# Output projection and first MLP unit of the second layer by token tile, and a later last query unit

## The reference

```python
# layer i = 1 of second_block
q, k, v = split_cols(h @ w, (ATT_QW, ATT_KVW, ATT_KVW))          # 16 query heads, 4 key heads, 64 wide
q = axial_rope(split_heads(q, ATT_Q_HEADS), row, col)            # a rotation by position
...
y = merge_heads(window_attention(q, k, v, k_c, v_c, od_sink[j])) @ od_w_out[j]   # 1024 x 1024
x = layer_norm(DEEPNORM_ALPHA * x + g1 * y, ln_g[i, 0], ln_b[i, 0])
m = jnp.square(jax.nn.relu((x * (1.0 + sc2) + sh2) @ mlp_w1[i])) @ mlp_w2[i]     # 1024 -> 4096 -> 1024
x = layer_norm(DEEPNORM_ALPHA * x + g2 * m, ln_g[i, 1], ln_b[i, 1])
```

## Time and profile before

| | |
|---|---|
| median of 3 runs | 1339.11 us |
| lowest and highest | 1335.56 and 1345.13 us |
| the profiled execution, its device time | 1340.16 us |
| its span in the trace | 1338.4 us |
| mean granted clock of TensorE | 0.991 |
| busy: PE, PEld, DVE, ACT, POOL | 97%, 90%, 66%, 43%, 8% |
| instructions | 24359 |

### The profile page before, as it was taken

How to read it: one execution, slowest core, us unless ns; L and a number is a source line. 1 busy time by engine, 2 the same in 40 slices (tenths; PEclk the granted TensorE clock), 3 DMA queues, 4 the chain that set the end, 5 groups by cost and what they waited for, 6 DMA issues and landing times.

```text
span 1338.4 us, 24359 instructions
## 1 busy us (share of the span) xinstructions
PE 1292.9 (97%) x10441; PEld 1205.1 (90%) x10441; DVE 883.2 (66%) x1357; ACT 579.2 (43%) x892; POOL 102.9 (8%) x153
## 2 busy tenths in 40 slices
PE   5899999999999999999999999999999899899997
PEld 4799998899988788899998898998999899899997
DVE  3567755557544466467677687676778886767566
ACT  4434445543665544526422313213155664445431
POOL 0111100000001111000000011111100120000000
PEclk9899999999989999999999999999999999999999
DMA  9897886445244544032444356575434202555550
GB/s 349 307 332 233 264 241 181 142 146 161 93 128 161 187 153 163 33 121 101 148 150 158 115 173 202 172 236 190 127 127 158 64 1 64 170 191 191 183 180 33
DMA packets 163881, 218.40 MB, mean 163 GB/s; under 512 B 6030, under 2 KB 141589, under 8 KB 163638
## 3 DMA queue, kind: packets, MB, share of 16 engines
q1 hardware_dynamic: 140196, 148.11, 33.7%
q0 software_dynamic: 22880, 67.42, 16.0%
q10 hardware_dynamic: 698, 1.32, 0.3%
HBM read 215.70 MB, written 1.12 MB: 162 GB/s over the span
## 4 chain that ended last, share of the span: by engine, by line
PE 84%; DVE 7%; DMA 4%; ACT 3%; issue 2%; POOL 0%; SPq 0%; DVEq 0%; ACTq 0%
PE bank L1322 30%; PE bank L694 11%; PE bank L713 10%; PE bank L746 7%; PE bank L729 4%; DMA strip_b<-distance_parts 2%; PE bank L1399 2%; PE bank L1226 2%; PE bank L887 2%; PE bank L805 2%; PE bank L1414 1%; PE bank L1300 1%; DVE wlo L2079 1%; DMA graw_b<-in_w_mod 1%; PE bank L998 1%
## 5 line engine op out<-in xcount | busy, mean ns | idle before, releaser
L2079 DVE TENSOR_TENSOR wlo<-raw,whi 128x2048 fp32r<-128x2048 f32 x131 | 297.4, 2275 | 93.5 <-ACT whi L1493 93.2
L1493 ACT ACTIVATE whi<-raw 128x2048 fp32r<-128x2048 f32 x131 | 247.9, 1898 | 194.7 <-PE bank L1322 130.9
L1322 PE MATMUL bank<-whi,m_hi 128*128 128x256 f32 x576 | 160.4, 278 | 1.2 <-DVE m_lo L2677 0.8
L1322 PE MATMUL bank<-whi,m_lo 128*128 128x256 f32 x576 | 159.7, 277 | 0.0
L1322 PE MATMUL bank<-wlo,m_hi 128*128 128x256 f32 x576 | 159.7, 277 | 0.0
L1322 PE MATMUL bank<-a_hi,whi 128*128 128x256 f32 (+1 forms) x448 | 148.5, 332 | 0.0
L1322 PE MATMUL bank<-a_lo,whi 128*128 128x256 f32 (+1 forms) x448 | 148.1, 331 | 0.0
L1322 PE MATMUL bank<-a_hi,wlo 128*128 128x256 f32 (+1 forms) x448 | 148.0, 330 | 0.0
L1322 PEld LDWEIGHTS bank<-whi,m_hi 128*128 128x128 f32 x576 | 108.5, 188 | 1.9 <-DVE m_lo L2677 1.2
L1322 PEld LDWEIGHTS bank<-whi,m_lo 128*128 128x128 f32 x576 | 108.3, 188 | 0.0
L1322 PEld LDWEIGHTS bank<-wlo,m_hi 128*128 128x128 f32 x576 | 108.1, 188 | 0.1
(11 more groups left out here) (439 smaller groups left out, 3335.3 us busy)
## 6 DMA issues: line engine op xcount, KB each, us to landing
raw<-in_mlp_w SPq DMA_DIRECT2D x64, 1024.0 KB, 5.2
raw<-in_w_in SPq DMA_DIRECT2D x32, 1024.0 KB, 7.2
graw_b<-in_w_mod POOLq DMA_DIRECT2D x64, 512.0 KB, 4.9
raw<-in_ev_w_in SPq DMA_DIRECT2D x12, 1024.0 KB, 5.1
pre<-in_w_ada SPq DMA_DIRECT2D x16, 512.0 KB, 9.8
graw_a<-in_w_mod POOLq DMA_DIRECT2D x16, 512.0 KB, 7.1
Y<-in_w_mod POOLq DMA_DIRECT2D x16, 512.0 KB, 4.2
raw<-in_od_w_qkv SPq DMA_DIRECT2D x6, 1024.0 KB, 4.8
```

The source lines that it names most:

```text
L1322: mm = nc.tensor.matmul(o, x, y, start=(k == 0 and i == 0), stop=(k == KT - 1 and i == 2))
L1493: nc.scalar.activation(split_pair(u, kt * cols)[0], landing(u, kt * cols), ACT.Copy).then_inc(hi_done, 1)
L2079: nc.vector.tensor_tensor(split_pair(u, n)[1], landing(u, n), bf(whi[u % HI], n), ALU.subtract).then_inc(lo_done, 1)
```

## The change

In the attention loop the last query unit moves. DVE rotates its two tiles in steps 4 and 5 (before: 1 and 3), PE transposes it in step 7 (before: 4), ACT and DVE round it in step 7 (before: 4). Its transpositions go to bank 0 instead of bank 1, so they wait for the first `window_out`, and the product with the values waits at `n` = 2 and `n` = 4 for what it did not wait for before.

After the attention, work goes by token tile. The projection is done as eight results of 24 matmuls, one for each unit and tile (`od_tile`); tile 0 of all four units comes first. Tile 0 is normalised while PE multiplies tile 1, its eight transpositions (`turn_tile(0)`) stand between the second and third result of tile 1, and the first MLP unit is multiplied for tile 0 (`first_hidden(0)`) before tile 1 is transposed, then for tile 1. That unit is therefore 96 matmuls of 128 columns instead of 48 of 256. `Y` rows 1 and 3 take the two normalised tiles, and `n_hi`, `n_lo` (in the place of `a_lo`) take what `a_hi`, `a_lo` took. ACT and DVE do their passes for each tile (`affine_tile`, `low_tile`: 128 x 128 instead of 128 x 256, twice as many), and the statistics for each tile and unit (`od_stats`). The splits of the weights change places too: `U_M1` and `U_M1 + 1` come between the tiles (the latter on DVE in four quarters, `quarter_lo`), and `U_M1 + 2` on ACT comes after tile 1's passes. The projection's weight buffers are all in use until tile 1 is multiplied, so `freed` for `U_OD` is four results later.

```diff
         for c0 in range(0, D, UC):
-            add(a["od_w_out_2"][0], c0, UC, 1)
+            add(a["od_w_out_2"][0], c0, UC, 2)
...
+        in_halves(U_OD, 4)
...
-        PAIRS, L_BANK, TQ_BANK = QH // 2 * NT, ((4, 5), (2, 3)), (6, 7, 0, 1)
+        PAIRS, L_BANK, TQ_BANK = QH // 2 * NT, ((4, 5), (2, 3)), (6, 7, 0, 0)
...
# PE, in transpose_q and window_values
+                if j == 3:
+                    pe.wait_ge(wa_o, 1)
...
-                if n < 4:
-                    pe.wait_ge(kq_ev, KVH + 3 + g)
+                if n in (0, 4):
+                    pe.wait_ge(kq_ev, KVH + 3 + g // 2)
+                elif n == 2:
+                    taken(pe, before[U_QKV + 5])
                 elif n % 2 == 0:
                     pe.wait_ge(wa_o, g - 1)
...
# PE, the attention loop
-                if n in (2, 4):
-                    transpose_q(1 + n // 2)
+                if n in (2, 7):
+                    transpose_q(2 if n == 2 else 3)
...
# PE, projection to MLP: all of it new
+            def first_hidden(m):
...
+                for n in range(2):
+                    for k in range(KT):
+                        if n == 0:
+                            pe.wait_ge(tr_lo, LN_T0[4] + KT * m + k + 1)
+                        for i, (w, x) in enumerate(((wh, n_hi), (wl, n_hi), (wh, n_lo))):
+                            mm = nc.tensor.matmul(bank[bk(b)][:, n * S + m * P:n * S + (m + 1) * P], w[:, k, n * P:(n + 1) * P],
+                                                  x[:, k, ms], start=(m + n + k + i == 0), stop=(k == KT - 1 and i == 2),
+                                                  skip_group_check=True)
...
+            for j in range(4):
+                od_tile(j, 0)
+            od_tile(0, 1)
+            od_tile(1, 1)
+            turn_tile(0)
+            od_tile(2, 1)
+            od_tile(3, 1)
+            first_hidden(0)
+            turn_tile(1)
+            first_hidden(1)
...
# ACT
-                if n in (3, 4):
-                    take_transposed(3 + n)
+                if n in (3, 7):
+                    take_transposed(6 if n == 3 else 7)
...
-            for u in range(U_OD, U_M1):
-                split_hi(u + LEAD)
-            tile_roots(4)
-            affine_half(4, 0)
+            split_hi(U_OD + LEAD)
+            tile_root(4, 0)
+            split_hi(U_M1)
+            act.wait_ge(aff_done, 3 + LN_CALL.index(4))
+            affine_tile(0)
+            split_hi(U_M1 + 1)
+            tile_root(4, 1)
+            affine_tile(1)
+            split_hi(U_M1 + 2)
...
# DVE
-                if n == 1:
-                    query_rows(3, (0,))
...
-                if n in (3, 4):
-                    low_transposed(3 + n)
-                if n == 3:
-                    query_rows(3, (1,))
+                if n in (3, 7):
+                    low_transposed(6 if n == 3 else 7)
+                if n in (4, 5):
+                    query_rows(3, (n - 4,))
...
+            split_lo(U_OD + LEAD)
+            for j in range(4):
+                od_stats(j, 0)
+            tile_norm(0)
+            od_stats(0, 1)
+            split_lo(U_M1)
+            od_stats(1, 1)
+            for k in range(KT):
+                low_tile(0, k)
+            od_stats(2, 1)
+            od_stats(3, 1)
+            tile_norm(1)
+            for k in range(KT):
+                low_tile(1, k)
+                if k % 2:
+                    quarter_lo(U_M1 + 1, k // 2)
+            split_lo(U_M1 + 2)
             residual(2, 0)
             residual(2, 1)
```

More of the change, by code:

```diff
@@ L273, in build @@
             o_hi, o_lo = [flat(a_hi)[:, i * 2048:(i + 1) * 2048].rearrange("p (k n) -> p k n", k=KT) for i in range(2)]
+            n_hi, n_lo = [flat(a_lo)[:, i * 2048:(i + 1) * 2048].rearrange("p (k n) -> p k n", k=KT) for i in range(2)]
             sink, nsink = stat[:, 44:60], stat[:, 24:40]
@@ L1456, in _ @@
             pe.wait_ge(wa_o, PAIRS // 2)
[L1457 to L1464, removed]
-                for k in range(KT):
[L1466 to L1469, removed]
@@ L1470, in _, with od_tile @@
-            for m in range(NT):
+            def od_tile(j, m):
+                u, b = U_OD + j, place[U_OD + j, m]
+                wh, wl = [w.rearrange("p (k n) -> p k n", k=KT) for w in split_pair(u)]
+                pe.wait_ge(lo_done, u + 1)
+                pe.wait_ge(free[bk(b)], nth(b))
+                for k in range(KT):
+                    for i, (w, x) in enumerate(((wh, o_hi), (wh, o_lo), (wl, o_hi))):
+                        mm = nc.tensor.matmul(bank[bk(b)][:, 0:UC], x[:, k, m * P:(m + 1) * P], w[:, k, :],
+                                              start=(k == 0 and i == 0), stop=(k == KT - 1 and i == 2))
+                mm.then_inc(tile_done, 1)
@@ L1477, in _ @@
-            col_half(U_M1, 0, a_hi, a_lo, before[U_M1], t0=LN_T0[4])
-            M1_ARGS = (U_M1, a_hi, a_lo, S, *half_m, 32, False)
+                    nc.tensor.transpose(bank[4 + k // 2][:, (k % 2) * S + m * P:(k % 2) * S + (m + 1) * P],
+                                        Y[:, 2 * m + 1, k * P:(k + 1) * P], ident).then_inc(tr_full, 1)
+            def first_hidden(m):
+                u, b = U_M1, before[U_M1]
+                wh, wl = [w.rearrange("p (k n) -> p k n", k=KT) for w in split_pair(u)]
+                pe.wait_ge(lo_done, u + 1)
+                if m == 0:
+                    pe.wait_ge(free[bk(b)], nth(b))
+                ms = slice(m * P, (m + 1) * P)
+                for n in range(2):
[6 more added lines that the diff above has]
+                                                  skip_group_check=True)
+                if m:
+                    mm.then_inc(tile_done, 1)
@@ L2059, in _ @@
             mlp(U_M1, S, half_m[0], 32, 3, lead=8 - LEAD)
-            tile_roots(6)
+            for m in range(NT):
+                tile_root(6, m)
         @block_.vector
@@ L2856, in _, with od_stats @@
             affine(4, 2, M1 + 24, M1 + 32).then_inc(aff_done, 1)
-            for u in range(U_OD, U_M1 - 1):
-                split_lo(u + LEAD)
-                gated_stats(before[u], grow[5][:, 0], xres, u - U_OD, 0, ALPHA)
-            for m in range(NT):
-                if m == 0:
-                    dve.wait_ge(od_half, 1)
-                b = before[U_M1 - 1]
-                tile_stats((take(b) if m else bank[7])[:, 0:UC], grow[5][:, 0], m, ALPHA, b if m else None)
-            for m, finished in enumerate((ln_even, ln_odd)):
+            def od_stats(j, m):
+                b = place[U_OD + j, m]
+                tile_stats(take(b)[:, 0:UC], grow[5][:, 0], m, ALPHA, b, j)
```

61 lines of the change are left out of this document (43 added, 18 removed).

## The result

The changed kernel takes 1342.22 us (median of 20 runs, 1338.74 to 1345.12) against 1339.25 us for the kernel before (20 runs, 1335.56 to 1345.13). The ratio is 1.002, 95% interval 1.0011 to 1.0029: 2.7 us slower, 1.5 to 3.9. By the measure of 1% that is no change. The profiled execution has 1342.75 us, its span 1340.9 us.

The account below looks back on a forecast made before the run. PE has 84% of the chain, but ACT and DVE hold up the start of the MLP. 1340.16 - 1.1 (attention) + 2.8 (projection to MLP) = 1341.9 us profiled, 1340.8 us median; range 1335.5 to 1345.0.

Parts of the forecast that it names:

- (a): Projection to MLP: PE fills its wait and becomes the bound, faster; -3.9 with the attention, 1335.2 us; chance 0.1.
- The attention: Attention loop: PE no longer waits for the second rotation, gains 1.9 us, gives part back; -1.1 us, between 0 and -1.9.
- The prices: Projection to MLP: 0.111 us per 128-column matmul, 0.59 per ACT `k` of 128 columns, 1.4 per tile and unit of statistics.
- rival (b): `affine_tile(1)`: tile 1's passes cost ACT what 256 columns cost; +1.4 us on the forecast, 1342.2; chance 0.12.
- rival (e): Second transpositions: the norm of tile 1 is what is late, 128-column matmuls being cheap; 1339.4 us; chance 0.08.
- The first square: Start of the MLP: first square 42.4 us after the projection's start instead of 39.64, +2.8 us.
- the term: Projection to MLP: +2.8 us; ends +1.3 (norm of tile 1 late) and +4.2 (ACT's passes at the 256-column price).
- Those 2.7 us are PE's slack.: MLP unit 4: PE ready near 58.0 us after projection start, fourth hidden unit at 60.7, so PE does not delay it.
- rival (c): `first_hidden(1)`: TensorE at its lower clock, 1.2 GHz, slower; 60 such matmuls give +3.3 us on the forecast, 1344.1; chance 0.06.
- Behind 1178.47 the change moves nothing: From the second part of MLP unit 4 on, where the chain returns to PE for good: no change in time.
- (d): Attention: DVE is late in every step and all the gain is given back; +1.1 us on the forecast, 1341.9; chance 0.14.

Follow-up runs that it names:

- wide_narrow: Changed kernel with the first MLP unit multiplied over all 256 columns ahead of tile 1's turn, then over tile 1's 128 behind it; ratio 1.0015.
- narrow_wide: Changed kernel with the first MLP unit multiplied over tile 0's 128 columns (thrown away), then over all 256 behind tile 1's turn; ratio 1.0001.
- att_only: Kernel before with the attention part of the change alone (last query unit rotated and transposed later); 1336.27 us, ratio 0.9986.
- reorder: Changed kernel, 96 narrow matmuls kept, with the rounding of `U_M1 + 2` and the two residual calls moved into idle ACT and DVE time; ratio 1.0023.
- wide_twice: Changed kernel with its 96 matmuls in the same places but each over 256 columns, the first 48 thrown away; ratio 1.0012.

## Why the prediction was right, and where it was wrong

The predicted time, 1340.8 us, lies 1.4 us under the median, within the range, and the class (no change by 1%) is the measured one. The forecast difference was +1.7 us, the measured one is +2.7. That the number came so near is partly luck: by the dates of the first profile of either kernel the change costs 4.5 us from the first logits on, mostly because one step failed. And the range was set by the scatter of three executions; every rival but (a) lay inside it too, so it could not have told them apart.

**The attention: right.** Predicted -1.1 us, measured -0.91 against the first profile. Counted from the first logits, the product with the values of pair 0 starts 1.76 us earlier than before (1.9 predicted), that of pair 2 1.60 us, and that of pair 3, which stands behind the transpositions of step 7, 1.22 us: the gain and most of what is given back are where the prediction had them. Not foreseen was that the removed wait is also one behind which the clock can fall (-2.5 then).

**The prices: right.** The 128-column matmul was put at 0.111 us and took 5.31 / 48 = 0.111. By the 81 ns of the Trainium skill, "TensorE: Matmul & The Clock Gate", section "Back-to-back issue gap", a tile would take an estimated 3.9 us; the measured 5.31 us decides against it for these matmuls. ACT's `k` over 128 columns was put at 0.59 us and took 0.54 (1148.23 to 1148.77), so rival (b) was wrong. The norm of tile 1 was put at S + 26.9 and was ready at 1144.29, S + 26.8; PE came at S + 28.4 (predicted 28.2), so rival (e) did not happen. The first square was put at S + 42.4 and came at 42.0. One end of the term was added up wrongly: with the norm late at S + 26.9 instead of 28.2 it would be +1.5, not +1.3. Nothing else rests on it.

**The step that failed: "Those 2.7 us are PE's slack."** It held PE at 2.4 GHz. PE should have ended `first_hidden(1)` at S + 37.3 and ended at S + 40.3; the three hidden units took 18.43 us where 144 x 0.115 = 16.6 were counted. Together 4.8 us, 2.7 of them slack, so 2.1 on the path: the second part of unit 4 starts at 62.8 instead of 60.7. That is rival (c), which had a chance of 0.06. Its mechanism was described rightly, and its arithmetic (slack first, then the path) too; it was judged unlikely by the wrong row. The argument against it was a stretch of the attention with PE busy 2.66 of 4 us at clock 1.00. The stretch 1150.40 to 1153.40 of the same group, at the very place that the change edits, stood at 0.50 with 256 columns, and `wide_narrow` and `narrow_wide` show that in the new order 128 columns there bring some 10 us at 0.50, and 256 none at that place. The nearest row was the one to go by. Two profiles of the kernel before that differ in the attention show besides that one row at 1.00 proves little: it can be 0.57 in the next execution.

**What the sum did not have: +0.7.** "Behind 1178.47 the change moves nothing" was not quite right. A unit of 48 matmuls in the MLP takes either 5.45 or 5.66 us, and seven units 38.08 or 39.58. Chain of the changed kernel in the later rounds:

```profile
1221.49 5.45 PE bank L1302 x48
1226.94 38.08 PE bank L1324 x336
1265.03 5.66 PE bank L1302 x48
```

and of the kernel before:

```profile
1218.19 5.66 PE bank L1300 x48
1223.85 39.58 PE bank L1322 x336
1263.42 5.45 PE bank L1300 x48
```

The pace changes at each unit 4, in every round, at a granted clock of 1.00. Before and after are in opposite step, and each keeps its step in a second execution. From unit 4 of the first round to that of the last, before takes 132.5 us and after 133.8; 0.6 comes back in the last units. What sets the step is open: of the ten edited kernels some fall on the one and some on the other side, and no date here sorts them.

The terms against the kernel before: -0.9 (attention), +4.7 (unit 4 later), +1.3 and -0.6 (pace), +4.5 by the first profile and +2.9 by the second one, whose attention fell to the low clock. The measured difference is +2.7 (1.5 to 3.9).

**The other rivals.** (a), that PE fills its wait and all gets faster, was half true: PE did fill the wait at the norm, and became the bound, but because its clock fell and not because ACT and DVE kept up. (d), that DVE gives the attention's gain back in every step, is excluded by `att_only`.

## What to carry to other kernels

Before work is moved into a wait of TensorE, look at the granted clock of the place, and ask what the new matmuls are: narrow ones with weights of their own cost nearly as much time as wide ones here (0.111 us against 0.114 to 0.118), and behind them the clock was low for 10 us, so that PE's slack must be reckoned at both levels. When two limits lie a few microseconds apart, lifting one can show nothing (the new order alone moved the end of unit 4 by no more than its clock did, and with wide matmuls it was worth 1.9 us); test the one with the other lifted too. A removed wait on TensorE can be worth more than what the walk of the waits gives: here 0.9 us, and 2.5 against an execution in which the clock fell behind it.

## What the runs showed of the hardware

- 48 fp32r matmuls of 128 columns, each with weights of its own, took 5.31 us (0.111 each), against 5.45 or 5.66 for 48 of 256 columns.
- With nearly equal busy time and waits of PE, the granted clock stayed at 1.00 with 256 columns behind the second turn and fell to 0.50 for some 10 us with 128 (13.7 in `reorder`); at 0.50 a 128-column matmul came every 0.222 us.
- Behind one and the same wait of 2.10 us the clock was 1.00 in one profile of the kernel before and 0.57 in another; this is 1.6 us of the attention. In unit 4 a wait of 1.88 us was followed by some 3.4 us at 0.50 (`narrow_wide`) and one of 1.72 us by none (`wide_twice`).
- The MLP's matmuls run at two paces, 0.1135 and 0.118 us, that alternate by round at full granted clock. The cause was not found.
